# Delta-rule inverses: one product per level instead of two, the second form turned by VectorE out of PSUM

## The reference

```
k_beta = k * beta[..., None]
L = jnp.where(strict, jnp.einsum("bhncd,bhnsd->bhncs", k_beta, k) * decay, 0.0)
a_mat = L + jnp.eye(CHUNK, dtype=f32)
rhs = jnp.concatenate([v_beta, k_beta * jnp.exp(g)[..., None]], axis=-1)
sol = lax.linalg.triangular_solve(a_mat, rhs, left_side=True, lower=True, unit_diagonal=True)
u, w = sol[..., :Dv], sol[..., Dv:]
```

## Time and profile before

| | |
|---|---|
| three runs | 1168.79 us median, 1166.94 to 1171.67 |
| profiled execution | 1167.02 us, span 1165.2 us |
| TensorE busy | 1118.7 us, 96% of the span |
| VectorE / ScalarE / GpSimd busy | 504.2 / 520.0 / 371.0 us |
| mean granted TensorE clock | 0.992 of full |

### The profile page before, as it was taken

One profiled execution on the slowest core, in us unless ns is written; L12 is line 12 of the kernel. 1 busy time (PEld: TensorE's weight loads), 2 busy tenths in 40 slices (PEclk: granted clock), 3 DMA queues, 4 the chain that ended last, 5 costly groups with the idle time before them and its releaser, 6 DMA issues.

```text
span 1165.2 us, 21348 instructions
## 1 busy us (share of the span) xinstructions
PE 1118.7 (96%) x8978; PEld 881.2 (76%) x8978; DVE 504.2 (43%) x894; ACT 520.0 (45%) x911; POOL 371.0 (32%) x148
## 2 busy tenths in 40 slices
PE   5999999999989999999999999999999999999998
PEld 3688886777768889777777667888877777778767
DVE  4575553453423457234134883753112332331562
ACT  5232326663425534453355893433235434753540
POOL 0134433132336441343433001333343223433260
PEclk8999999999999999999999999999999999999999
DMA  9822331286751122324532100313222421224201
GB/s 316 263 73 77 103 108 38 71 262 206 226 183 39 38 73 73 109 73 126 133 104 73 37 1 23 123 56 108 91 77 71 115 83 57 88 73 158 99 1 73
DMA packets 103007, 119.38 MB, mean 102 GB/s; under 512 B 4679, under 2 KB 89207, under 8 KB 102791
## 3 DMA queue, kind: packets, MB, share of 16 engines
q1 hardware_dynamic: 99054, 115.08, 31.1%
q10 hardware_dynamic: 3864, 3.01, 0.9%
HBM read 110.75 MB, written 2.10 MB: 97 GB/s over the span
## 4 chain that ended last, share of the span: by engine, by line
PE 83%; ACT 6%; DVE 4%; issue 3%; DMA 1%; ACTq 0%; SPq 0%; POOL 0%; DVEq 0%
PE ps L2072 43%; PE ps L2865 4%; PE ps L2118 2%; PE ps L2460 2%; PE ps L2213 2%; PE ps L2675 2%; PE ps L2710 2%; PE ps L2156 1%; PE ps L2693 1%; PE ps L2236 1%; PE ps L2289 1%; PE ps L2831 1%; PE ps L2487 1%; PE ps L2818 1%; DMA ada_a<-in_w_ada_dram 1%
## 5 line engine op out<-in xcount | busy, mean ns | idle before, releaser
L610 POOL TENSOR_TENSOR wlo<-raw,whi 128x2048 fp32r<-128x2048 f32 x53 | 245.3, 4628 | 527.6 <-ACT whi L776 515.1
L776 ACT ACTIVATE whi<-raw 128x2048 fp32r<-128x2048 f32 x52 | 99.3, 1911 | 192.2 <-PE ps L2072 152.6
L616 POOL TENSOR_TENSOR wlo<-raw,whi 128x2048 fp32r<-128x2048 f32 x10 | 46.4, 4641 | 110.9 <-ACT whi L865 62.7
L1802 DVE TENSOR_TENSOR_SCAN taken<-kept,taken 128x255 f32<-128x255 f32 (+2 forms) x64 | 51.2, 853 | 21.4 <-ACT taken L1196 21.4
L1286 ACT ACTIVATE p<-sc,nmx 128x256 f32<-128x256 f32 x64 | 32.0, 501 | 45.8 <-PE ps L2818 44.7
L1899 DVE CUSTOM_DVE_ANT_0 sc<-ps,biast 128x256 f32<-128x256 f32 (+1 forms) x64 | 22.4, 393 | 65.7 <-PE ps L2807 36.7
L865 ACT ACTIVATE whi<-raw 128x2048 fp32r<-128x2048 f32 x11 | 21.1, 1918 | 62.7 <-PE ps L2072 62.7
L2072 PE MATMUL ps<-hC_hi,whi 128*128 128x512 f32 x184 | 47.0, 397 | 0.8 <-POOL wlo L610 0.8
L2072 PE MATMUL ps<-hC_lo,whi 128*128 128x512 f32 x184 | 45.5, 390 | 0.0
L2072 PE MATMUL ps<-hC_hi,wlo 128*128 128x512 f32 x184 | 45.4, 389 | 0.0
L2072 PEld LDWEIGHTS ps<-hC_hi,whi 128*128 128x128 f32 x184 | 33.7, 188 | 14.8 <-issue 6.4
(11 more groups left out here) (506 smaller groups left out, 2682.5 us busy)
## 6 DMA issues: line engine op xcount, KB each, us to landing
raw<-in_w_in_dram SPq DMA_DIRECT2D x24, 1024.0 KB, 5.2
raw<-in_w_in_a_dram SPq DMA_DIRECT2D x16, 1024.0 KB, 5.6
raw<-in_w_ada_dram SPq DMA_DIRECT2D x8, 1024.0 KB, 5.2
late_w<-in_w_ada_dram SPq DMA_DIRECT2D x8, 1024.0 KB, 5.5
raw<-in_w_kv_dram SPq DMA_DIRECT2D x8, 1024.0 KB, 5.2
raw<-in_w_in_b_dram SPq DMA_DIRECT2D x8, 1024.0 KB, 5.4
ada_a<-in_w_ada_dram SPq DMA_DIRECT2D x4, 1024.0 KB, 10.2
ada_b<-in_w_ada_dram SPq DMA_DIRECT2D x4, 1024.0 KB, 13.0
```

The source lines that it names most:

```text
L610: pool.tensor_tensor(wlo[:, s, :], raw[:, s, :], whi[:, s, :].bitcast(F32), ALU.subtract).then_inc(lo_ready, 1)
L616: pool.tensor_tensor(wlo[:, s, :], raw[:, s, :], whi[:, s, :].bitcast(F32), ALU.subtract).then_inc(lo_ready, 1)
L776: A(whi[:, s, :], raw[:, s, :], ACT.Copy).then_inc(hi_ready, 1)
L1802: last = dve.tensor_tensor_scan(taken[:, r % 3, keys], kept[:, r % 3, keys], taken[:, r % 3, keys], 0.0, ALU.mult, ALU.add)
```

## The change

The second product of a level (L2487) goes. TensorE makes only X transposed, of head 2p in bank 2 and of head 2p+1 in bank 6, and VectorE makes X from it: `dve.transpose` reads the bank in PSUM and turns it by blocks of 32 x 32, which is enough as long as the inverted blocks are no larger than 32. ACT copies only the transposed form, per head, and waits for the transposes of its level. Y is in bank 0 for head 2p and bank 1 for head 2p+1, and each step of a level is split by head with a semaphore increment of its own. All products of the levels go from half n to half n, `XT` stays in its own half (`inverse_moved` is one operation of 128 partitions), `keys_scaled` is one operation, and values are now exchanged for heads 4 to 7, no longer for heads 0 to 3.

```
 # DVE
-                    dve.wait_ge(y_full, 5 * p + lv + 1)
                     dve.wait_ge(yi_init, 5 * p + lv + 1)
-                    dve.copy_predicated(even(yib[:, (p + lv) % 2, :, :], b),
-                                        mask.unsqueeze(1).broadcast_to([128, 2 * NT, 32 // b, b]),
-                                        even(both(0), b)).then_inc(yi_done, 1)
+                    for s in range(2):
+                        dve.wait_ge(y_full, step(p, lv, s) + 1)
+                        dve.copy_predicated(even(yib[:, (p + lv) % 2, 4 * s:4 * s + 4, :], b),
+                                            mask.unsqueeze(1).broadcast_to([128, NT, 32 // b, b]),
+                                            even(half_bank(s, 0), b)).then_inc(yi_done, 1)
...
+                    if lv < 4:
+                        for s in range(2):
+                            dve.wait_ge(xn_full, step(p, lv, s) + 1)
+                            dve.transpose(xin[:, (2 * p + s) % 4, :, :], half_bank(X_BANKS[s], 0)).then_inc(xin_turned, 1)
 # ACT
-                    act.wait_ge(xn_full, 5 * p + lv + 1)
-                    if lv < 4:
-                        A(even(of_pair(xin, 2 * p % 4), b), even(both(1), b), ACT.Copy).then_inc(x_evac, 1)
-                    A(odd(of_pair(XT, 2 * p), b), odd(both(2), b), ACT.Copy).then_inc(x_evac, 1)
+                    for s in range(2):
+                        if lv < 4:
+                            act.wait_ge(xin_turned, 8 * p + 2 * lv + s + 1)
+                        act.wait_ge(xn_full, step(p, lv, s) + 1)
+                        A(odd(XT[:, 2 * p + s, :, :], b), odd(half_bank(X_BANKS[s], 0), b), ACT.Copy).then_inc(x_evac, 1)
...
-                for n in range(2):
-                    last = A(XT[side(1 - n), h, :, :], x0[side(n), h % 4, :, :], ACT.Copy)
-                last.then_inc(xt_moved, 1)
+                A(XT[:, h, :, :], x0[:, h % 4, :, :], ACT.Copy).then_inc(xt_moved, 1)
 # PE
-                tokens_down(v_bank(h), 16 + h, h < HG // 2).then_inc(v_tp, 1)
+                tokens_down(v_bank(h), 16 + h, h >= HG // 2).then_inc(v_tp, 1)
...
-                        pe.wait_ge(xin_done, 2 * p + 2)
-                    else:
-                        pe.wait_ge(x_evac, 9 * p + 2 * lv - 1)
                     for s in range(2):
+                        if lv == 0:
+                            pe.wait_ge(xin_done, 2 * p + s + 1)
+                            if s and p:
+                                pe.wait_ge(w_evac, 2 * p - 1)
+                            elif s:
+                                pe.wait_ge(v_evac, 2)
+                        else:
+                            pe.wait_ge(xin_turned, 8 * p + 2 * (lv - 1) + s + 1)
                         for i, n in TILES:
-                            last = mm(block64(0, s, i, 1 - n), ntm[side(n), (2 * p + s) % 4, i, :],
+                            last = mm(block64(s, 0, i, n), ntm[side(n), (2 * p + s) % 4, i, :],
                                       xin[side(n), (2 * p + s) % 4, i, :], start=True, stop=True)
-                    last.then_inc(y_full, 1)
+                        last.then_inc(y_full, 1)
...
-                    pe.wait_ge(yi_done, 5 * p + lv + 1)
...
                     for s in range(2):
+                        pe.wait_ge(yi_done, step(p, lv, s) + 1)
+                        if lv == 0:
+                            pe.wait_ge(xt_moved, 2 * p + s + 1)
+                        else:
+                            pe.wait_ge(x_evac, step(p, lv - 1, s) + 1)
                         for i, n in TILES:
-                            xt, yi = XT[side(n), 2 * p + s, i, :], yib[side(n), (p + lv) % 2, 4 * s + i, :]
-                            if lv < 4:
-                                mm(block64(1, s, i, 1 - n), xt, yi, start=True, stop=True)
-                            last = mm(block64(2, s, i, n), yi, xt, start=True, stop=True)
-                    last.then_inc(xn_full, 1)
+                            last = mm(block64(X_BANKS[s], 0, i, n), yib[side(n), (p + lv) % 2, 4 * s + i, :],
+                                      XT[side(n), 2 * p + s, i, :], start=True, stop=True)
+                        last.then_inc(xn_full, 1)
```

More of the change, by code:

```diff
@@ L419, in mixer_stack @@
         os_done, mc_done, roots_moved = sem("os_done"), sem("mc_done"), sem("roots_moved")
-        beta_done, xt_moved = sem("beta_done"), sem("xt_moved")
+        beta_done, xt_moved, xin_turned = sem("beta_done"), sem("xt_moved"), sem("xin_turned")
         x_tile = [sem(f"x_tile{i}") for i in range(NT)]
@@ L464, in of_pair, with step @@
             return ap[:, h:h + 2, :, :].rearrange("p h i n -> p (h i) n")
+        def step(p, lv, s):
+            return 10 * p + 2 * lv + s
         W_BANKS = ((6, 1), (3, 2))
+        X_BANKS = (2, 6)
         FOLD_BANKS = (4, 5, 7, 6)
@@ L655, in restores @@
                     if lv >= 2:
-                        pool.wait_ge(xn_full, 5 * p + lv - 1)
+                        pool.wait_ge(xn_full, 2 * (5 * p + lv - 1))
                     elif p:
-                        pool.wait_ge(xn_full, 5 * (p - 1) + lv + 4)
+                        pool.wait_ge(xn_full, 2 * (5 * (p - 1) + lv + 4))
                     restore(p, lv)
@@ L987, in _ @@
                     for n, bank in enumerate(W_BANKS[s]):
-                        last = A(qkvT[:, 8 + h, :].rearrange("p (i c n) -> p i c n", c=2, n=CH)[:, :, half_of(h, 1 - n), :],
+                        last = A(qkvT[:, 8 + h, :].rearrange("p (i c n) -> p i c n", c=2, n=CH)[:, :, half_of(h, n), :],
                                  half_bank(bank, 0), ACT.Copy, scale=-1.0)
@@ L1535, in keys_scaled @@
                     dve.wait_ge(w_full, h - 3)
[L1536 to L1539, removed]
+                TT(kbg[:, h % 4, :, :], ps[:, k_bank(h), :].rearrange("p (i n) -> p i n", i=NT),
+                   heads(gt[:, 10, :])[:, :, h].unsqueeze(2).broadcast_to([128, NT, 128]), ALU.mult).then_inc(k_evac, 1)
             def decay_exponents(h):
@@ L1555, in first_inverse @@
                 if h >= 4:
-                    dve.wait_ge(y_full, 5 * (h // 2 - 1))
+                    dve.wait_ge(y_full, 10 * (h // 2 - 1))
                 for i in range(NT):
@@ L2478, in _ @@
                         else:
[L2479 removed]
                             pe.wait_ge(kd_evac, 2)
[L2481 to L2482 removed]
+                            pe.wait_ge(gate_dve, 11)
                     for s in range(2):
[L2484 to L2489 removed]
+                        pe.wait_ge(yi_done, step(p, lv, s) + 1)
[3 more added lines that the diff above has]
+                            pe.wait_ge(x_evac, step(p, lv - 1, s) + 1)
+                        for i, n in TILES:
+                            last = mm(block64(X_BANKS[s], 0, i, n), yib[side(n), (p + lv) % 2, 4 * s + i, :],
+                                      XT[side(n), 2 * p + s, i, :], start=True, stop=True)
+                        last.then_inc(xn_full, 1)
                     filler(2 if lv == 4 or nxt is not None and lv < 3 else 1)
@@ L2492, in _ @@
                     h = 2 * p + s
-                    pe.wait_ge(x_evac, 9 * p + 9)
+                    pe.wait_ge(x_evac, step(p, 4, 1) + 1)
                     if h == 0:
@@ L2504, in _ @@
             late_columns()
-            pe.wait_ge(x_evac, 9 * (HG // 2))
+            pe.wait_ge(x_evac, 10 * (HG // 2))
             pe.wait_ge(w_evac, HG)
@@ L2526, in chunk_values @@
                         h = k if n == c else 4 + k
-                        last = mm(ps[side(n), c, 128 * k:128 * k + 128], XT[side(1 - n), h, i, :], V[side(1 - n), i, h, :],
+                        last = mm(ps[side(n), c, 128 * k:128 * k + 128], XT[side(n), h, i, :], V[side(n), i, h, :],
                                   start=k == 0, stop=i == 0 and c == 0, skip_group_check=True)
```

4 lines of the change are left out of this document (removed).

## The result

| | before | after |
|---|---|---|
| median of the runs | 1169.12 us (6 runs, 1166.94 to 1171.67) | 1159.93 us (6 runs, 1158.67 to 1163.45) |
| profiled execution | 1167.02 us, span 1165.2 | 1159.38 us, span 1157.6 |
| ratio, 95% interval | | 0.9921, 0.9900 to 0.9942 |

The change makes the kernel faster by 0.8%, 9.2 us. The two profiled executions differ by 7.6 us; the other 1.6 us of the medians' difference no trace places.

What follows compares the result with a forecast made beforehand. TensorE was taken to set the time, busy 104.6 of the stage's 116 us. Terms 0 - 0.8 + 1.3 + 1.4 - 1.4 - 1.1 = -0.6 us gave a median of 1168.2 us, range 1163 to 1172.5.

Steps and rivals of the forecast that it cites:

- E: TensorE's waits for instructions in the stage, 6.4 us: 4 of 23 packets fewer take off 1.1 us.
- A to D: The four terms for pair 0's start, exchanged values, VectorE's level 3 queue and pair 3: together +0.5 us.
- The removed product: Second product of a level: ran beside the one that stays in otherwise unused array quarters, so its removal gives 0.
- A: Start of pair 0: head 0's Y fills the wait for head 1's xin, head 2's values are plain transposes; -0.8 us.
- B: Values of heads 4 to 7 are now exchanged, 0.43 us each, partly inside waits before the gates; +1.3 us.
- C: Level 3 of pairs 0 to 2: VectorE's queue delays its transposes, so Y waits 0, 0.9 and 0.5; +1.4 us.
- D: Pair 3, no work between: TensorE's waits at level 0 and at the end mostly go; -1.4 us.
- rival 2: TensorE's instruction stream no longer runs dry: all 6.4 us of issue waits go, 1162.9 us; chance 0.14.

Runs made afterwards that it cites:

- e1: The kernel before without the second product of a level (L2487), ScalarE copying xin's new blocks from bank 2: 1162.81 us, ratio 0.9944.
- e4: The kernel before with transfers of modulation units from number 8 on cut from 1 MB to 128 KB: 1160.93 us, ratio 0.9937.
- after_again: The changed kernel measured once more, unaltered, beside other versions: 1160.61 us, ratio to before 0.9911.
- e2_products_back: The changed kernel with a second product put back beside each one that stays, written to PSUM nobody reads: 1176.86 us, ratio to before 1.0054.
- e3_transposes_first: The changed kernel with VectorE's first inverse of head 2p+3 moved behind the transposes of level 3, into level 4: 1161.62 us, ratio to before 0.9927.

## Why the prediction was wrong

The step that failed is term E, the stalls: the prediction priced them at 6.4 us, took 1.1 of that off in proportion to packets, and so gave the change -1.1 where the runs show -9.0. The time failed with it. The measured sizes of A to D are differences of the stretches between the first Y of each pair, with the stalls taken off: from the stage's start to pair 1 29.95 us against 32.32 - 1.93, pair 1 26.47 against 26.03 - 0.72, pair 2 26.47 against 29.90 - 4.67, pair 3 to `chunk_values` 18.77 - 1.08 against 21.97 - 2.81. Point by point:

- **The removed product: 0.** Right. 1.08 us for 32 where 64 took 1.09, and e1's rest of 99.8 against 100.1.
- **A, -0.8.** Measured -1.3: the half Y fits (-0.55) and the wait shrinks to 1.11. The plain values of head 2 gave -0.59 for the -0.43 taken. The +0.2 expected at head 3 didn't come: its gates wait 0.74 instead of 0.24, yet from that Y to their end it took 3.98 us where it had taken 4.07.
- **B, +1.3.** Measured +0.6 to +0.7, a little under its bound of +0.8: exchanging the values of a head costs 0.29 more than turning them plainly, since the 32 MATMULs of a head's values and keys take 1.90 from the first start to the next step where 0.59 + 1.02 stood before; the 0.43 was the difference of these two. The wait of 0.25 before the gates went as said, so a pair pays 0.29 + 0.04.
- **C, +1.4.** Measured +2.6: the mechanism and the place are right, 0.9 per pair as worked out for pair 1 (a wait of 0.81 and the 0.07 of overlap that it ends), but in all three pairs. For pair 0 I had let a stall hide it and for pair 2 a shorter operation; the stall was gone, and the operation of the earlier trace rows took 0.84 in each of the three. Why it did, and what that is worth, stands below. The price of the transpose from PSUM was 0.439 for the 0.43 taken.
- **D, -1.4.** Measured -1.4 to -1.5.
- **A to D** come to +0.5 measured and +0.5 predicted, with errors that cancel.
- **E, -1.1, bounds -6.4 and +1.9.** Measured -9.0 (10.1 to 1.1), outside the bounds. The term also left out the weights' transfers; with small ones the same instructions lose 1.7 us (e4). Three things were wrong in what it had. The stalls were sized by the waits view, 6.4 us, while the steps in which they lie were 10.1 us too long: the view leaves out the lengthening inside a group and the stretch at 1.2 GHz behind the stall of 1.87. The gain was taken in proportion to packets, 4 of 23, while a stall appears only where instructions are used up before the next packet is there, and can go altogether: with 4 packets fewer one stall of six is left. And against rival 2 I held that the longest stall lay in a filler with few records. That was a misreading twice over. The earlier trace rows has a longer wait, 2.2 us, in front of a Y (336.80), so the bound of +1.9, one more like the longest, was too small as well. And the place of a stall is only where the instructions ran out: right before the filler, at 316.8, and again at 332.9, stood a step of 128 records in 1.1 us.

Why the operation of the earlier trace rows took 0.84 can be read from GpSimd's rows. It is slow exactly when it starts inside GpSimd's reset of `yib`: it stands 88 times in the eleven profiled stages, 21 times it starts so and takes 0.76 to 0.88 us, and the other 67 times it takes 0.44 to 0.47. Pair 0 in the changed kernel, then in after_again:

```profile
267.65 0.61 POOL L630 COPY yib<-cs 128x512 f32<-128x512 f32 x1 [0.52 <-PE ps L2498]
267.72 0.84 DVE L1565 COPY_PREDICATED x<-cs,ntm 128x256 f32<-128x256 int32 x1
...
267.10 0.46 DVE L1565 COPY_PREDICATED x<-cs,ntm 128x256 f32<-128x256 int32 x1
267.12 0.88 POOL L630 COPY yib<-cs 128x512 f32<-128x512 f32 x1 [0.60 <-PE ps L2498]
```

In the second, VectorE was 0.02 us ahead and TensorE waited 0.32 instead of 0.81. The step behind which it waited was too long by 0.39 instead of 0.88, so in pair 0 a little over half of the price of C is this meeting, and the rest is VectorE's order. That it is the same in pairs 1 and 2 is likely, but no run shows it.

Of the prediction's sums, one is off: the bounds of A to D with E at -1.1 reach up to 1171.6, not to 1170.5. It didn't matter for the outcome.

Rival 2 was the mechanism, given 0.14 and 1162.9. With E at -9.0 and A to D at +0.5 the median before, 1168.8, becomes 1160.3, the result within its spread. The Trainium skill's page Runtime: NRT & Kernel Launch, Instruction fetch mechanics, calls the cost of crossing to the next block mostly hidden. In this stage before it was not: 10.1 of 110.2 us were lost. After the change the trace comes near the rule, with 1.1 of 101.7.

What stays open: why a stall falls in one execution and not in another (e1's runs spread from 1160.21 to 1169.10), what the long executions of e2_products_back lost, and the 1.0 us by which the changed kernel reached the stage later in its profile (0.4 in after_again's).

## What to carry to other kernels

An engine that looks full of products can be short of instructions. Where a stage on TensorE shows waits without a releaser, sum the excess length of whole steps rather than the waits, and ask how many instructions per us it uses and which large transfers run beside it; removing instructions that cost no time of their own can then bring time all the same, here 6.6 us for the removal alone. A wait that is repaired can be given back there, as in e3_transposes_first: the engine comes to the same packet sooner, and the packet doesn't.

## What the runs showed of the hardware

- Instruction packets of queue q8 take 0.96 to 1.13 us in the median of each kernel's stage, single ones 0.88 to 2.17. With 1 MB transfers the three compared packets began 1.6 to 3.1 us later than with 128 KB. In all 21 stalls of 0.4 us or more TensorE went on 2.4 to 2.7 us after the start of a packet (272.31 after 269.84 and 320.82 after 318.23 in the kernel before).
- Behind an idle time of 1.87 us the granted clock fell to 0.50 for about 3 us, in e1 behind one of 1.85 and in e2_products_back behind one of 2.57; after 1.85 and 2.17 in the kernel before, and after 2.25 and 2.60 in e2_products_back, it did not. Of the 11 idle times of 1.7 us or more in the profiled stages three were followed by it.
- Two products in different quarters of the array run free beside each other when alternated (1.09 us for 64 MATMULs) and cost 0.4 more when each head's eight stand in a row (1.49).
- A VectorE transpose of 128 x 256 float32 out of PSUM takes 439 ns, and 434 from SBUF.
- VectorE's masked copy into `x`, 128 x 256 float32, took 0.44 to 0.47 us in 67 of 88 cases and 0.76 to 0.88 in the 21 in which it started inside a copy by GpSimd. When VectorE was ahead by 0.02 us it was GpSimd's that grew, from 0.61 to 0.88.
